# The last gate tile in two halves inside the recurrence chain of a hybrid decoder layer, with other places for six norm turns, TensorE's waits and four VectorE steps

## What is computed

```
x = x + 0.5 * SwiGLU_1(RMSNorm(x))              FFN 1, hidden width 2816
P = RMSNorm(x) @ w_in                           26 tiles of 128 columns
o = concat[RWKV7(P), RGLRU(P), GatedDeltaNet(P), GLA(P)]
x = x + o @ w_out
x = x + 0.5 * SwiGLU_2(RMSNorm(x))              FFN 2
```

## Time and profile before

| what | us |
|---|---|
| median of three runs | 1408.76 |
| the profiled execution, its own time | 1409.95 |
| span of the profiled execution | 1408.2 |
| TensorE busy with matmuls in it | 1370.9 |
| VectorE busy | 857.6 |
| ScalarE busy | 679.2 |
| mean granted TensorE clock | 0.998 of 2.4 GHz |

### The profile page before, as it was taken

One profiled execution on the slowest core, in us unless ns is written; L12 is line 12 of the kernel. 1 busy time (PEld: TensorE's weight loads), 2 busy tenths in 40 slices (PEclk: granted clock), 3 DMA queues, 4 the chain that ended last, 5 costly groups with the idle time before them and its releaser, 6 DMA issues.

```text
span 1408.2 us, 31541 instructions
## 1 busy us (share of the span) xinstructions
PE 1370.9 (97%) x12556; PEld 1326.9 (94%) x12556; DVE 857.6 (61%) x1309; ACT 679.2 (48%) x938; POOL 74.0 (5%) x109
## 2 busy tenths in 40 slices
PE   7999999999999999999999999999999899999997
PEld 7999999889988999999999999998998789999997
DVE  6666534897676766653476664359975667666533
ACT  7454433835345645443374543356454456545332
POOL 0000000100020100000010000010001301000000
PEclk9999999999999999999999999999999999999999
DMA  8544444323212544444454444433232035444441
GB/s 294 164 149 149 149 149 149 105 67 101 63 47 80 191 163 149 149 149 146 145 185 148 149 148 150 149 124 104 77 91 77 19 133 168 149 148 149 150 149 51
DMA packets 50766, 185.87 MB, mean 132 GB/s; under 512 B 5760, under 2 KB 6272, under 8 KB 50176
## 3 DMA queue, kind: packets, MB, share of 16 engines
q1 hardware_dynamic: 49104, 177.37, 39.3%
q10 hardware_dynamic: 1584, 7.35, 1.4%
HBM read 180.14 MB, written 4.56 MB: 131 GB/s over the span
## 4 chain that ended last, share of the span: by engine, by line
PE 83%; DVE 12%; issue 2%; ACT 2%; DMA 0%; DVEq 0%; ACTq 0%
PE ps L465 25%; PE ps L467 24%; PE ps L466 24%; DVE xl L1484 2%; DVE wl L1462 2%; PE ps L771 1%; PE ps L759 1%; PE ps L797 1%; ACT wh L1102 1%; DVE x L1465 1%; DVE ar L1619 1%; PE ps L712 1%; PE ps L786 1%; PE ps L639 1%; DVE ar L1533 0%
## 5 line engine op out<-in xcount | busy, mean ns | idle before, releaser
L465 PE MATMUL ps<-xh,wh 128*128 128x320 f32 x1952 | 613.3, 314 | 14.7 <-DVE xl L1484 12.2
L1462 DVE TENSOR_TENSOR wl<-raw,wh 128x1024 fp32r<-128x1024 f32 x332 | 407.3, 1227 | 334.0 <-ACT wh L1102 333.5
L467 PE MATMUL ps<-xh,wl 128*128 128x320 f32 x1952 | 604.0, 309 | 0.0
L466 PE MATMUL ps<-xl,wh 128*128 128x320 f32 x1952 | 603.9, 309 | 0.0
L1102 ACT ACTIVATE wh<-raw 128x1024 fp32r<-128x1024 f32 x332 | 349.3, 1054 | 406.0 <-PE ps L467 401.0
L465 PEld LDWEIGHTS ps<-xh,wh 128*128 128x128 f32 x1952 | 367.2, 188 | 26.9 <-issue 8.7
L466 PEld LDWEIGHTS ps<-xl,wh 128*128 128x128 f32 x1952 | 367.4, 188 | 0.8
L467 PEld LDWEIGHTS ps<-xh,wl 128*128 128x128 f32 x1952 | 367.3, 188 | 0.0
L465 PE MATMUL ps<-hid_h,wh 128*128 (+1 forms) x704 | 217.9, 310 | 2.5 <-DVE hid_l L1509 2.5
L467 PE MATMUL ps<-hid_h,wl 128*128 (+1 forms) x704 | 217.5, 309 | 0.0
L466 PE MATMUL ps<-hid_l,wh 128*128 (+1 forms) x704 | 217.5, 309 | 0.0
(11 more groups left out here) (287 smaller groups left out, 981.8 us busy)
## 6 DMA issues: line engine op xcount, KB each, us to landing
raw<-wts SPq DMA_DIRECT2D x332, 512.0 KB, 3.5
ms<-mst ACTq DMA_DIRECT2D x2, 1440.0 KB, 8.4
mout<-ms ACTq DMA_DIRECT2D x2, 1440.0 KB, 6.6
x<-xT SPq DMA_DIRECT2D x4, 320.0 KB, 5.0
yT<-x SPq DMA_DIRECT2D x4, 320.0 KB, 2.2
cs<-cst SPq DMA_DIRECT2D x1, 652.0 KB, 8.6
pr<-par ACTq DMA_DIRECT2D x1, 429.0 KB, 4.4
pr<-par ACTq DMA_DIRECT2D x1, 425.0 KB, 5.2
```

The lines of the kernel that those rows point to most:

```text
L465: pe.matmul(out, a, rh, start=start, stop=False)
L466: pe.matmul(out, a, rl, start=False, stop=False)
L467: return pe.matmul(out, b, rh, start=False, stop=stop)
L1462: tt(wl[:, s, :], raw_of(layer, n), wh[:, s, :].bitcast(F32), ALU.subtract).then_inc(lo_ready.sem, 1)
```

## The change

- `norm_tiles` takes the first three tiles in turns for six slices, not four; the norm's sum stands behind tile 2, not tile 1.
- TensorE's waits by `on` are plain waits, no longer `apart`.
- TensorE: the two halves of tile 25 leave their places around `gla_level(4)` and go into round 0 of the chain, one behind `r_products(0)`, one behind `u_products(0)`. `gla_states` goes behind `m_products(0)`; `gla_within` and `gla_decode` behind `r_products(1)`.
- ScalarE: `ahead(25)` moves from ahead of the copy of GLA's rows into round 2, behind the gelu.
- VectorE: `evac(25)` moves from ahead of `take(5)` to behind `g_m(0)`; `ahead(25)` from round 0 to round 2, behind `g_u(2)`; `rw_shift` from round 1 to behind `ahead(24)`, ahead of `take(3)`; `centering` from round 1 into round 3; `inverse(0, 1)` stands ahead of `ahead(12)`.

```diff
--- before.py
+++ after.py
@@ -52,7 +52,7 @@
             + [GLA0 + 128 * i for i in range(4)] + [RG0 + 128 * i for i in range(2)]
             + [GDN0 + 3 * GW + 128 * i for i in range(2)] + [GLA0 + 128 * i for i in range(4, 6)]
             + [RG0 + 128 * i for i in range(2, 4)])
-LATE = 14
+LATE, TURNS = 14, 6
 
 
 def raw_places():
@@ -374,7 +374,7 @@
                 S[name] = signal(name, n)
 
         passed = signal("passed")
-        OWN_WAITS = (mybir.EngineType.PE, mybir.EngineType.Pool)
+        OWN_WAITS = (mybir.EngineType.Pool,)
 
         def apart(eng, s, value):
 
@@ -521,14 +521,14 @@
                     return three(ps[:, m, 0:TOK], *wsl(slot(layer, base + m), k), xh[:, k, :], xl[:, k, :], k == 0, k == KT - 1)
 
                 early = range(RING - 1)
-                for k in range(KT // 2):
+                for k in range(TURNS):
                     for m in early:
                         part(m, k)
                 for m in early:
-                    for k in range(KT // 2, KT):
+                    for k in range(TURNS, KT):
                         ins = part(m, k)
                     ins.then_inc(unit_used.sem, 1)
-                    if m == 1:
+                    if m == RING - 2:
                         norm_sums(layer, which)
                 for k in range(KT):
                     ins = part(RING - 1, k)
@@ -907,13 +907,15 @@
                                 into(2, DEC, p, b, Mgla[r, 1 + q, :], lqe[r, SEQ + q * DECT:SEQ + (q + 1) * DECT], q * DECT, DECT)
 
                 r_products(0)
+                half_tile(layer, 25, 0)
+                u_products(0)
+                half_tile(layer, 25, 1)
+                m_products(0)
+                gla_states()
+
+                r_products(1)
                 gla_within()
-                u_products(0)
-                gla_states()
-                m_products(0)
                 gla_decode()
-
-                r_products(1)
                 gla_between()
                 u_products(1)
                 known(DEC)
@@ -1054,9 +1056,7 @@
                 rg_gate(layer, 1)
                 gla_level(layer, 3)
                 inverse_y(layer, 1, 4)
-                half_tile(layer, 25, 0)
                 gla_level(layer, 4)
-                half_tile(layer, 25, 1)
                 inverse_t(layer, 1, 5)
                 gla_level(layer, 5)
                 inverse_y(layer, 1, 5)
@@ -1337,7 +1337,6 @@
                 st(act.activation(lkd, lkd, ACT.Exp, scale=1.0 / GLA_TAU))
                 say(act.activation(lB, lB, ACT.Exp, scale=1.0 / GLA_TAU), "leB")
                 inverse_t(1, 5)
-                ahead(25)
                 on(act, layer, "gla_rows_mm")
                 say(act.activation(lkt[:].rearrange("q c p t -> q p c t"),
                                    ps[:, 6:8, 0:NC * DK].rearrange("q p (c t) -> q p c t", c=NC), ACT.Copy), "gla_rows")
@@ -1384,6 +1383,7 @@
                 act.preload_act_table_set("gelu_apprx_tanh_and_others")
                 r_evac("rU", UU[0], 2)
                 say(act.activation(rgg[:], rgg[:], ACT.Gelu_apprx_tanh), "gates")
+                ahead(25)
                 m_evac(2)
 
                 r_evac("rR", RR[0], 3)
@@ -1854,6 +1854,11 @@
                     if l < 5:
                         turn(g, blocks(l))
 
+                def rw_shift():
+
+                    for p in range(2):
+                        st(stt(rw_bonus[:, p, :], rw_bonus[:, p, :], P("lnb", p), rw_g[:, p, :], ALU.add, ALU.mult))
+
                 def recurrences():
 
                     def centering():
@@ -1891,9 +1896,9 @@
 
                     g_r(0)
                     rg_steps()
-                    ahead(25)
                     g_u(0)
                     g_m(0)
+                    evac(25)
                     gla_chain()
 
                     g_r(1)
@@ -1901,8 +1906,6 @@
                     rg_root(1)
                     g_u(1)
                     rg_root(2)
-                    rw_shift()
-                    centering()
                     g_m(1)
                     on(ve, layer, "silus")
                     on(ve, layer, "ysq2")
@@ -1918,6 +1922,7 @@
 
                     g_r(3)
                     rg_out()
+                    centering()
                     g_u(3)
                     g_m(3)
                     dec_add(2)
@@ -1934,11 +1939,6 @@
                         say(tt(y[:], y[:], rw_bonus[:], ALU.add), "o_ready")
                     else:
                         say(tt(y[:], (gz if g == 1 else gt)[:], ysq[g][:], ALU.mult), "o_ready")
-
-                def rw_shift():
-
-                    for p in range(2):
-                        st(stt(rw_bonus[:, p, :], rw_bonus[:, p, :], P("lnb", p), rw_g[:, p, :], ALU.add, ALU.mult))
 
                 def gated(g):
 
@@ -2029,8 +2029,8 @@
                 ahead(11)
                 gdn_conv(2)
                 evac(12)
+                inverse(0, 1)
                 ahead(12)
-                inverse(0, 1)
                 rw_gain()
                 gdn_conv(3)
                 evac(13)
@@ -2088,13 +2088,13 @@
                 evac(24)
                 gla_last()
                 ahead(24)
+                rw_shift()
                 take(3)
                 inverse(1, 4)
                 take(4)
                 gla_reads(5)
                 gla_reads(6)
                 gla_ends()
-                evac(25)
                 take(5)
                 inverse(1, 5)
                 take(6)
```

## The result

The changed kernel takes 1410.87 us (median; 1409.40 to 1412.33) beside 1408.81 us for the kernel before in the same job: ratio 1.0016, 95% interval [1.0009, 1.0023]. It is 2.3 us slower by this ratio (2.1 by the medians), where 2.6 us faster were forecast; its own profiled execution took 1410.84 us around a span of 1409.0.

A forecast was written before the change was run, and what follows sets the result against it. TensorE, busy 1370.9 of 1408.2 us, was taken to bound the kernel, so only its gaps could change. Openings -2.3, inverse -1.9, joined waits -0.8 and chain +2.4 gave -2.6 from 1408.8: 1406.2 us, range 1402.8 to 1410.2.

The forecast's parts named there:

- Six turns: Norm openings: all `xl` waits but the first go, part of the gain lost to later `rstd`; -2.3 us.
- VectorE's `inverse(0, 1)`: Mixer, ahead of `ahead(12)`: TensorE's 0.94 us wait for the transpose goes in both layers; -1.9 us.
- Joined waits: TensorE's waits joined to the instruction behind: 0.09 us saved for each that binds; -0.8 us, bounds 0 to -2.
- Before the chain: Chain starts at 402.4, not 403.4, 1.0 us gained; the halves' old places cost 2.9 us of new waits.
- Round 0 and 1: Chain start to second `m_products`' first half: new path 10.5 + 3.9 + g, against 12.49 and 15.28 us before.
- g: Gaps of "issue" left in the new path of rounds 0 and 1; taken as 0.9 us, bounds 0 and 3.
- Round 2: `m_products(1)` to `gM` takes 9.6 us: -0.1 and +1.4 by layer; TensorE waits up to 2 us at `r_products(3)`.
- The chain's sum: Chain part over both layers: layer 0 +1.7, layer 1 +0.4, moved load +0.3, together +2.4 us.
- the first: Rival: instruction fetch relieved altogether, g = 0 and no collision with the moved load; 1404.1 us, chance 0.29.
- the second: Rival: fetch loses more, the moved load hitting round 3 and g 2.5 behind the halves; 1412.3 us, chance 0.13.
- the third: Rival: the gaps are no fetches and stay, 1.9 us in layer 0, 3.5 in layer 1; 1409.5 us, chance 0.12.
- the fourth: Rival: nothing is kept, openings give no lead and joined waits nothing; 1409.3 us, chance 0.06.

The follow-up runs named there:

- P: D with VectorE's `rw_gain` moved ahead of `ahead(12)`: 1396.88 us, 0.9921 of the kernel before.
- B: The kernel before with TensorE's waits joined to the instruction behind, alone: 1401.35 us, ratio 0.9953.
- H: The changed kernel with tile 25's first half back ahead of level 4, the second still in the chain: 1407.04 us, 0.9989 of the kernel before.
- I: The changed kernel with both halves of tile 25 back at their old places around level 4: 1402.52 us, 0.9955 of the kernel before.
- D: The kernel before with six turns and later norm sum, joined waits and `inverse(0, 1)` ahead of `ahead(12)`, without the chain part: 1398.14 us, ratio 0.9932.
- E: D with the fourth output tile's split later, on ScalarE behind the gelu and on VectorE behind `g_m(2)`: 1397.92 us, 0.9928 of the kernel before.
- C: The kernel before with the chain part alone (four turns, separate waits, old order at `ahead(12)`): 1414.76 us, ratio 1.0057.
- A: The kernel before with six turns and the later norm sum alone: 1406.36 us, ratio 0.9990.
- K: The changed kernel with tile 25's first half worked out twice, an extra thrown away ahead of level 4: 1409.69 us, 1.0012 of the kernel before.
- J: I with VectorE's split of the fourth output tile behind `g_m(2)` in place of `g_u(2)`: 1400.98 us, 0.9943 of the kernel before.
- S: D with VectorE's bonus shift ahead of the chain and the centering in round 3: 1396.43 us, 0.9918 of the kernel before.

## Why the prediction was wrong, step by step

The sum was -2.3 - 1.9 - 0.8 + 2.4 = -2.6. The runs give -1.4 - 1.6 - 6.6 + 11.9 = +2.3. Two terms failed, with opposite signs, and the larger of them decides: the chain part, put at +2.4, cost 11.9.

- **Six turns: right.** -2.3 forecast. By the trace the five openings together got 2.7 us shorter in the changed kernel: all waits for `xl` but the first gone; 283.59 came only 0.30 us earlier, with a wait of 1.59 in place of 0.59; layer 1's mixer lost 0.75 where 0.85 were forecast; the fifth tile of the FFNs waits 0.3. In the run of their own they brought 1.4 us [0.1 to 2.7], which takes in both.
- **VectorE's `inverse(0, 1)`: half right.** The wait at L759 went, but "late next would be the split of tile 16" was wrong: it is `rw_gain`, left behind the split of tile 12, for which L678 waits 0.40 us. By the trace 0.54 us are kept in each layer, not 0.95. P shows it: with the gain moved along the wait is gone. I had followed the tiles behind the moved step, not the next thing in VectorE's own queue.
- **Joined waits: mis-sized, -0.8 forecast, -6.6 measured** (bounds 0 to -2). The 0.09 us for a wait that binds was read rightly, and "waits that don't bind cost nothing visible" holds (the idle extra waits cost 0). What failed is the count of consequences: held waits of their own go with 4.7 us of gaps that joined ones don't have, and with the one fall of the clock at 1108.15, which B is without. I had these gaps in the sum, but under the chain part.
- **Before the chain: the start right, its reasons not.** Forecast 402.4, measured 402.62. But TensorE arrived 0.84 us earlier, so nothing was gained where 1.0 was forecast: the four groups above took 1.19 us longer at the low clock. "The halves' old places thus cost 2.9 us of new waits" was right in kind, and should have been the alarm. 3.9 us of free work went where it isn't free; H and I price it at 8.6 us with what follows from it. The traces say the same: from D to the changed kernel the span grows by 12.8 us (1396.2 to 1409.0), and layer 0's chain starts no earlier for the halves' absence (402.46 and 402.62), so 7.8 of the 12.8 are the halves' own matmuls, no longer under waits; the rest is the low clock and the new waits.
- **Round 0 and 1: g was right, the clock wrong.** No gap of issue stands between the halves, so g = 0, better than the 0.9 taken, and 14.4 us were due. But from the chain's start to ScalarE's state update behind `m_products(1)` layer 0 took 15.4 us (402.62 to 418.02) and layer 1 16.3 (1097.03 to 1113.30) for 15.3 forecast, as the low clock took back what g gave, and in layer 1 more. "The clock fell right behind that gap and shouldn't then": this sentence is the failed one. It was right that the gap of 1.94 us goes; the new waits of 1.34 and 0.94 us, with small matmuls between them, came with a fall of twice the length in both layers. What that costs in layer 1 is the difference of 10.09 and 8.28 us in round 0 alone.
- **Round 2: right.** A wait "up to 2 us" for `gM`; 1.67. From `m_products(1)` to `gM` 9.6 us were forecast and layer 0 took 9.45 (418.02 to 427.47). Behind it, in layer 0, a further fall of the clock that I had not foreseen. The +0.3 for the moved load isn't seen: E is as fast as D.
- **The chain's sum, +2.4 for +11.9.** The two misses meet here: the baseline. I set the new chain against 12.49 and 15.28 us, with their gaps. With joined waits the baseline has next to no gaps: D's chains take 26.14 and 26.23 us, and the changed kernel's 32.79 and 32.33. D's, in windows as above:

```profile
402.46:428.60 26.14, 23.80 (x703) 21.11 (x697) 18.52 (x48) 14.52 (x27) 9.33 (x11) 1.00 0.12 32
1090.33:1116.56 26.23, 23.74 (x702) 21.11 (x697) 18.60 (x48) 14.51 (x27) 9.26 (x11) 1.00 0.10 31
```

Of the rivals none happened. The gaps went altogether, as the first has it, and the time still rose; the second has the right side and a wrong mechanism (no gap of issue is left in the view); the third falls with B and C, which remove the gaps; the fourth falls with A and B, which gain 1.4 and 6.6 us. Nearly every sign that was to show the forecast's case came: the wait at 283.59, none for the transpose, waits of 2 to 3 us ahead of the chain, no gap between the halves, 1.67 us for `gM`. None of them was a sign of the clock or of the baseline, so they could all come true beside a wrong sum. The measured 1410.9 lies over the range's 1410.2, since no case in it had the clock fall more often than before.

What stays open: why in H the clock still falls ahead of the chain, though its waits there are 0.33 and 1.41 us, and why in K, with the same waits in both layers, it falls ahead of layer 0's chain and holds ahead of layer 1's; and how the 3.1 us by which J's span is over S's divide between the two waits shown above (1.7 us in each layer) and the rest.

## What to carry to other kernels

Before work is moved out of a stretch, ask what it covers: here wide matmuls between steps of a ping-pong with VectorE were free, and the clock fell less with them; in a stretch bound by TensorE they cost their full time. When two edits remove the same gaps, take the second one's price against the kernel with the first in. And when a step is pulled ahead of another, look at everything behind both in that engine's queue, not only at the waits that the trace shows now.

## What was not expected of the hardware

- Waits of TensorE as instructions of their own: 0.09 us each by release to start, but 6.6 us over the kernel, 4.7 of them in gaps that the profile puts down to issue. The 82 idle ones that were added in the chains cost nothing that can be told.
- In layer 0, with a wait of 1.34 us, 32 small matmuls, a wait of 0.30, 32 more and then a wait of 0.94 us, TensorE went to 1.2 GHz for 6.83 us. Groups of 32 small matmuls take 1.06 us there and 0.62 at 2.4 GHz. The Trainium skill's "TensorE: Matmul & The Clock Gate", part 1, says that activity is what releases the throttle. K agrees in the main: with 3.9 us of added work the clock was low for 10.2 us in place of 17.1, and the time did not rise; but in layer 0 it still fell ahead of the chain.
